# A two-block layer kernel: the norm's factor ahead of the MLP applied to the gate and up results, input blocks made within the output product

## The reference

```python
def rms_norm(x, g):
    xf = x.astype(jnp.float32)
    y = xf * lax.rsqrt(jnp.mean(xf * xf, axis=-1, keepdims=True) + EPS)
    return (y * g.astype(jnp.float32)).astype(x.dtype)
...
    h = h + m @ w_o
    hn = rms_norm(h, norm2_g)
    gate, up = jnp.split(hn @ w_gate_up, 2, axis=-1)
    return h + (jax.nn.silu(gate) * up) @ w_down
```

## Time and profile before

| | us |
|---|---|
| median of 3 runs | 2365.99 |
| lowest, highest | 2365.02, 2367.89 |
| the profiled execution, its own time | 2365.47 |
| its span in the profile | 2363.7 |
| TensorE busy, share of the span | 2202.0, 93% |
| mean granted clock of TensorE, share of full speed | 0.969 |

### The profile page before, as it was taken

How to read it: one execution, slowest core, us unless ns; L and a number is a source line. 1 busy time by engine, 2 the same in 40 slices (tenths; PEclk the granted TensorE clock), 3 DMA queues, 4 the chain that set the end, 5 groups by cost and what they waited for, 6 DMA issues and landing times.

```text
span 2363.7 us, 29779 instructions
## 1 busy us (share of the span) xinstructions
PE 2202.0 (93%) x10756; PEld 1811.1 (77%) x10756; DVE 1410.7 (60%) x2782; ACT 899.4 (38%) x1609; POOL 1003.0 (42%) x575
## 2 busy tenths in 40 slices
PE   7999999999999989999589999999999798998896
PEld 6877688998887767788368888888888576878774
DVE  4258799999902566661646666665467617307713
ACT  5234522232225754431422333334455333226622
POOL 1355433465452332144465454555488513130042
PEclk9999999999999989999789999999999899999998
DMA  5111111111242121243124444447855121110212
GB/s 181 52 45 68 55 53 52 47 45 45 74 131 90 63 80 37 72 152 124 55 87 156 157 156 157 154 152 251 298 168 169 54 107 36 54 45 15 90 41 89
DMA packets 235366, 233.74 MB, mean 99 GB/s; under 512 B 10194, under 2 KB 177775, under 8 KB 235231
## 3 DMA queue, kind: packets, MB, share of 16 engines
q1 hardware_dynamic: 231072, 218.77, 28.5%
q10 hardware_dynamic: 4158, 13.16, 1.4%
HBM read 169.82 MB, written 61.15 MB: 98 GB/s over the span
## 4 chain that ended last, share of the span: by engine, by line
PE 72%; DVE 9%; ACT 3%; issue 2%; POOL 2%; DMA 1%; SPq 0%; ACTq 0%; DVEq 0%
PE ps L889 23%; PE ps L1177 17%; PE ps L1199 9%; PE ps L1242 8%; PE ps L1066 6%; PE ps L1388 4%; PE ps L1098 1%; POOL xl_P L2836 1%; DVE logit L2106 1%; PE ps L1041 1%; PE ps L1084 1%; ACT p_s L1928 1%; DVE pt_lo L2125 1%; DVE mix L2282 0%; PE ps L1311 0%
## 5 line engine op out<-in xcount | busy, mean ns | idle before, releaser
L2645 POOL TENSOR_TENSOR w_lo<-w_raw,w_hi 128x1024 fp32r<-128x1024 f32 (+1 forms) x135 | 290.8, 2155 | 887.7 <-ACT w_hi L1420 887.7
L889 PE MATMUL ps<-x_hi,w_hi 128*128 128x512 f32 (+2 forms) x960 | 361.6, 377 | 3.3 <-DVE c_rs L2023 3.3
L889 PE MATMUL ps<-x_lo,w_hi 128*128 128x512 f32 (+2 forms) x960 | 360.1, 375 | 0.0
L889 PE MATMUL ps<-x_hi,w_lo 128*128 128x512 f32 (+2 forms) x960 | 358.1, 373 | 0.0
L1177 PE MATMUL ps<-xh_P,wr_hi 128*128 128x512 f32 x616 | 246.5, 400 | 29.9 <-issue 21.9
L1177 PE MATMUL ps<-xl_P,wr_hi 128*128 128x512 f32 x616 | 245.7, 399 | 0.0
L1177 PE MATMUL ps<-xh_P,wr_lo 128*128 128x512 f32 x616 | 245.5, 399 | 0.0
L889 PEld LDWEIGHTS ps<-x_hi,w_hi 128*128 128x128 f32 x960 | 181.7, 189 | 39.1 <-issue 8.4
L889 PEld LDWEIGHTS ps<-x_hi,w_lo 128*128 128x128 f32 x960 | 181.9, 190 | 28.9
L889 PEld LDWEIGHTS ps<-x_lo,w_hi 128*128 128x128 f32 x960 | 181.6, 189 | 28.4
L1420 ACT CAST w_hi<-w_raw 128x1024 fp32r<-128x1024 f32 (+1 forms) x135 | 127.1, 943 | 171.3 <-PE ps L889 83.4
(11 more groups left out here) (405 smaller groups left out, 4910.2 us busy)
## 6 DMA issues: line engine op xcount, KB each, us to landing
w_raw<-in_w_in SPq DMA_DIRECT2D x74, 512.0 KB, 3.6
wdr<-as_scratch SPq DMA_DIRECT2D x77, 256.0 KB, 3.3
rawg<-in_w_gate_up SPq DMA_DIRECT2D x22, 512.0 KB, 3.9
rawu<-in_w_gate_up SPq DMA_DIRECT2D x22, 512.0 KB, 5.3
wdr<-in_w_down SPq DMA_DIRECT2D x22, 512.0 KB, 6.5
as_scratch<-ac SPq DMA_DIRECT2D x44, 256.0 KB, 3.8
wt_scratch<-wdr SPq DMA_DIRECT2D x33, 256.0 KB, 5.0
as_scratch<-a SPq DMA_DIRECT2D x33, 256.0 KB, 3.5
```

What stands on the lines that cost most here:

```text
L889: mm = pe.matmul(ps[:, b, 0:n], w[:, s, P * k:P * k + P], r[:, k, t0:t0 + n], start=k == 0 and i == 0, stop=k == kd - 1 and i == 2 and ext ...
L2645: pool.tensor_tensor(w_lo[:, p % 2, 0:n], w_raw[:, p % 2, 0:n], w_hi[:, p % 2, 0:n], ALU.subtract).then_inc(wlo_done, 1)
```

## The change

- The inputs of the product are no longer multiplied by the norm's factor. ACT scales a tile of `mix` by the gain only (`gained`, in place; the last tile into `gh7`) once SP's store of it has landed (`park_sum`), and does so within the output product, one panel behind. The squares are made by half tile, and summed over tiles in `rsb[0]` and `rsb[1]`.
- Casts of the tiles of P1 and P2 (`x_high`), their low parts and the four sums of each tile pair (`sums`) stand within the output product too; `combined_weights(0)` and six `block_low` are there as well. The sums reuse other tiles than before. The blocks are placed elsewhere, and `xtr` has two buffers instead of four.
- TensorE sums and spreads the squares in one step (two matmuls of `ones` with `rsb`, behind P2 of pair 0). DVE makes the mean and the reciprocal on 128 x 512 numbers (`inverse_rms`), ACT the root, within pair 0.
- In each pair P2 is multiplied by `rsb[0]` ahead of its silu (DVE, `gate`), `g1` by `rsb[1]` ahead of its silu (DVE), and `a[1]` and `a[0]` by `rsb[1]` and `rsb[0]` ahead of the multiplication with `g1` and `g0` (POOL).
- `down_combined(0)` moves from pair 0 to pair 1.

```diff
@@ TensorE
-            norm_sums(0)
-            norm_spread(0)
...
                     if prod == "P7":
-                        pe.wait_ge(po_done, 5 * n + 1)
+                        pe.wait_ge(po_done, 7 * n + 1)
...
+                    if n == 0 and prod == "P2":
+                        pe.wait_ge(acca_done, 14)
+                        for h in range(2):
+                            pe.matmul(ps[:, 6 + h, :], ones[:, :], rsb[h][:, :], start=True, stop=True).then_inc(rs_full, 1)
@@ ACT
+            def gained(m):
+
+                act.wait_ge(park_store[m % 2], PARK_0[m % 2] + 16 * (m // 2 + 1))
+                act.wait_ge(sqa_done, 2 * m + 2)
+                act.activation(mix[:, m, :], mix[:, m, :], ACT.Copy, scale=v("norm2_g", m)).then_inc(hn_done, 1)
...
+                square(m, 0)
+                if m:
+                    gained(m - 1)
+                    x_high(m - 1)
...
+                    if n == 0 and i == 3:
+                        act.wait_ge(nst_step, 4)
+                        for h in range(2):
+                            act.activation(rsb[h][:, :], rsb[h][:, :], ACT.Sqrt).then_inc(nrt_done, 1)
+                    if i == (at("P2") + 1 if n else 5):
+                        act.wait_ge(po_done, 7 * n + 2)
+                        act.activation(g0[:, :], g0[:, :], ACT.Silu).then_inc(sil_done, 1)
@@ DVE
+            def sums(k):
+                dve.wait_ge(hn_done, scaled_at(4 + k))
+                dve.tensor_tensor(wdr[:, k, :], scaled(k, 1), scaled(4 + k, 1), ALU.add).then_inc(s0_done, 1)
...
+            def inverse_rms():
+                for h in range(2):
+                    dve.wait_ge(rs_full, h + 1)
+                    dve.tensor_scalar(rsb[h][:, :], ps[:, 6 + h, :], 1.0 / D, EPS, ALU.mult, ALU.add).then_inc(nst_step, 1)
+                for h in range(2):
+                    dve.wait_ge(nst_step, h + 1)
+                    dve.reciprocal(rsb[h][:, :], rsb[h][:, :]).then_inc(nst_step, 1)
...
+                def gate():
+                    if n:
+                        dve.wait_ge(am_done, AM_DONE_0 + 4 * n)
+                    else:
+                        dve.wait_ge(nrt_done, 2)
+                    dve.wait_ge(blk_done, BLK_DONE_0 + 7 * n + at("P2") + 1)
+                    dve.tensor_tensor(g0[:, :], bank_of["P2"], rsb[0][:, :], ALU.mult).then_inc(po_done, 1)
...
+                        dve.tensor_tensor(g1[:, :], g1[:, :], rsb[1][:, :], ALU.mult).then_inc(po_done, 1)
@@ POOL
-                    if i == 3 and n % 2 == 0:
+                    if (n, i) == (1, 1) or i == 3 and n % 2 == 0 and n:
                         down_combined(n // 2)
                     if i == 5:
+                        pool.wait_ge(po_done, 7 * n + 4)
+                        pool.tensor_tensor(a[1][:, :], a[1][:, :], rsb[1][:, :], ALU.mult).then_inc(am_done, 1)
+                        pool.wait_ge(am_done, AM_DONE_0 + 4 * n + 1)
                         pool.wait_ge(sil_done, 2 * n + 2)
                         pool.tensor_tensor(a[1][:, :], a[1][:, :], g1[:, :], ALU.mult).then_inc(am_done, 1)
                     if i == 6:
-                        pool.wait_ge(po_done, 5 * n + 5)
+                        pool.wait_ge(po_done, 7 * n + 7)
+                        pool.tensor_tensor(a[0][:, :], a[0][:, :], rsb[0][:, :], ALU.mult).then_inc(am_done, 1)
+                        pool.wait_ge(am_done, AM_DONE_0 + 4 * n + 3)
                         pool.tensor_tensor(a[0][:, :], a[0][:, :], g0[:, :], ALU.mult).then_inc(am_done, 1)
```

More of the change, by code:

```diff
@@ L325, in build @@
         gy_s = place("gy_s", [P, 2, BANK], F32, ST + 20 * S)
-        n_acc = place("n_acc", [P, 1, S], F32, ST)
-        n_sq = place("n_sq", [P, 2, 2, S], F32, ST + 8 * S)
+        n_sq = place("n_sq", [P, 2, BANK], F32, ST + 8 * S)
+        rsb = [place("rsb0", [P, BANK], F32, RA + 30 * S), place("rsb1", [P, BANK], F32, W_RAW + 6 * KD * P * 4 + 32 * S)]
+        gh7 = place("gh7", [P, S], F32, ST + 24 * S)
         n_diag2 = place("n_diag2", [P, S], F32, ST + 8 * S)
@@ L668, in half, with scaled, scaled_at, sum_at @@
             return slice(BANK * h, BANK * h + BANK)
+        def scaled(m, h):
+            return gh7[:, half(h)] if m == KD - 1 else mix[:, m, half(h)]
+        def scaled_at(m, h=1):
+            return HN_DONE_0 + m + 1 + (h if m == KD - 1 else 0)
+        SUMS = ("S1", "S3", "S2", "S4")
+        def sum_at(name, k):
+            return S0_DONE_0 + 4 * k + SUMS.index(name) + 1
+        def block_tile(y):
+            prod, k = FIRST[y // 4], y % 4
+            return prod, k, {"P1": scaled(k, 0), "P2": scaled(4 + k, 0), "P4": scaled(4 + k, 1), "P5": wdr[:, k, :],
+                             "P6": scaled(k, 0), "P7": scaled(k, 1), "P3": scaled(4 + k, 0)}[prod]
+        IN_SET = {"P1": 1, "P2": 1, "P6": 0, "P7": 0, "P5": 3, "P3": 3, "P4": 2}
         block = ctx.enter_context(nc.Block())
@@ L758, in _ @@
                     sp.wait_ge(olo_done, 8)
-                    for n in range(4):
-                        load_residual(n)
+                    load_residual(0)
+                    load_residual(1)
                 if kind == "wo" and m >= 4:
-                    load_residual(2 * m - 4)
-                    load_residual(2 * m - 3)
+                    load_residual(2 * m - 6)
+                    load_residual(2 * m - 5)
+                    park_sum(m - 4)
                 if key == ("wo", 1):
@@ L769, in _ @@
                     load_pair(0)
[L771 to L775, removed]
+            for m in range(4, KD):
+                if m < KD - 1:
+                    load_residual(2 * m + 2)
+                    load_residual(2 * m + 3)
+                park_sum(m)
             load_pair(1)
             def store_inner(j):
-                sp.wait_ge(am_done, AM_DONE_0 + 4 * j + 4)
+                sp.wait_ge(am_done, AM_DONE_0 + 8 * j + 8)
                 sp.wait_ge(ac_done, AC_DONE_0 + 4 * j + 4)
@@ L1798, in _ @@
                         block_high(q)
-            norm_split()
+            gained_last(1)
+            for y in range(8, 12):
+                x_high(y)
             for n in range(FC):
@@ L2279, in normalized @@
-            def normalized(z):
-                m, h = PIECES[z]
-                dve.wait_ge(rs_full, h + 1)
-                dve.scalar_tensor_tensor(out=mix[:, m, half(h)], in0=mix[:, m, half(h)], scalar=v("norm2_g", m), in1=ps[:, 6 + h, :],
-                                         op0=ALU.mult, op1=ALU.mult).then_inc(hn_done, 1)
-            dve.wait_ge(hs_store, 16 * KD)
-            for z in range(8):
-                normalized(z)
-            for y in (1, 3):
-                x_low(y)
```

288 lines of the change are left out of this document (147 added, 141 removed).

## The result

The changed kernel takes 2404.24 us (median of 4 runs, 2401.08 to 2406.75) against 2365.51 us of the kernel before on the same chip: ratio 1.0164, 95% interval 1.0146 to 1.0181. It is slower by 38.7 us; the prediction was 2402.0, range 2355 to 2422.

A forecast was written before the change was run, and what follows sets the result against it. TensorE, 93% busy, was taken to bound the kernel: only its gaps can give time, and new gaps are paid in full. 2365.5 - 13.9 - 7.2 + 57.6 = 2402.0 us, range 2355 to 2422.

The forecast's parts named there:

- Ahead of the pairs: From the output product's end through pair 0: 49.5 us instead of 63.45, -13.9 us, bounds -18 and -8.
- Pair 1: Second MLP pair: P7 has no wait, so 19.5 us instead of 26.7, -7.2 us, bounds -7.2 and -3.
- The ring: Dependency loop over two pairs: +5.85 us less 1.75 of slack makes P7 wait 4.1 us in odd pairs 3 to 19.
- a: POOL from down_combined to the low part of block 7n+12: 9.5 us, predicted to grow by 1.85.
- b: DVE's combined_weights and the sum of P6 behind it: 5.1 us, predicted to grow by 1.1.
- d: From the pair's end to POOL's low part of block 7n+6: 5.6 us, predicted to grow by 2.9.
- e: SP's load_pair and wdr loads, from that low part until POOL starts: 8.9 us, predicted unchanged.
- Piece c: TensorE's P7, P4 and P3 in the odd pair: 8.4 us, predicted unchanged.
- The turns of DVE and POOL: Inside the pairs, two-input DVE and POOL instructions alternate on one port: wait 4.1 us; without this 2.05.
- The clock: TensorE's clock falls anew behind each of nine P7 waits in odd pairs 3 to 19, costing 2.3 us each.
- Stalls, clock stays up: Rival: the nine P7 waits cost 4.1 us each without clock falls, 2381 us; chance 0.17.
- the pairs hold: Rival: inside the pairs additions stay under 1.5 us, P7 never waits, 2344.4 us; chance 0.17.

The follow-up runs named there:

- the run without the first wait: Changed kernel without TensorE's wait for all 16 half sums ahead of pair 0: 2403.43 us, ratio 1.0165.
- the one with the reciprocals moved: Changed kernel, pair 0: DVE's inverse_rms and gate moved behind the sum a[1] of P7, ACT's roots from i = 3 to i = 5: 2408.86 us, ratio 1.0179.
- The experiment one pair ahead of the waits: Changed kernel without POOL's two multiplications by rsb in the odd pairs: 2368.70 us, ratio 1.0014.
- the run without the factor: Changed kernel without POOL's two multiplications and DVE's one of g1 by rsb from pair 2 on: 2351.26 us, ratio 0.9953.
- exchanging two groups of DVE instructions: Changed kernel, from pair 1 on DVE adds P6 to r1 ahead of combined_weights for the next pair: 2364.41 us, ratio 1.0005.
- the sum first in the kernel before: Kernel before, from pair 1 on the sum of P6 put ahead of combined_weights: 2372.48 us, ratio 1.0013.
- the low part of block 15: Against the 2360.23 us version with reordered sums and roots: DVE makes pair 1's low part of block 15 behind the sums of P7; 2361.05 us, ratio 0.9972.
- `wdr` early: Changed kernel, SP issues the wdr loads of even pairs ahead of its low-part waits and load_pair: 2398.33 us, ratio 1.0148.
- the run without DVE's part: Changed kernel without DVE's multiplication of g1 by rsb[1] from pair 2 on: 2385.7 us, one run.

## Why the prediction was right, and where it was not

It was right in sign, in size (+36.5 us expected, +38.7 measured) and in its main mechanism, and some of the agreement is luck: three terms were off and partly cancelled.

- *Ahead of the pairs*: -13.9 expected, -10.2 measured (63.45 to 53.2). The mis-sized term is DVE's queue ahead of P7's sum, which ended 43.0 us after the product instead of 39.5; what stands behind it took 10.2 instead of 10. It was late from its start. The last half sum was done at 10.2 instead of 8.8, and the low parts of the input tiles up to the 19th at 24.9 (the row of 1161.80) instead of 20.6, several of them at 1.7 us each beside POOL's. The two reciprocals measured 6.54, as estimated (3.3 each) from the 6.65 of 1040 columns. Ahead of them DVE was idle for 1.77 us at 1167.51, waiting for ACT: ACT's casts of P7 stood behind the cast of block 7, which waited for `combined_weights(1)`. P1 also started later, at 10.3 instead of 8.9, which by itself cost nothing, as the run without the first wait shows. That run and the one with the reciprocals moved show that this whole part is one queue: taking one piece out frees little.
- *Pair 1*: 19.5 expected, 19.6 measured.
- *The ring*: the pieces were a +1.85, b +1.1, d +2.9, e 0. In pairs 6 to 8 they measure a +1.7 (11.2 against 9.5), b +1.0 (6.1 against 5.1), d +2.3 (7.9 against 5.6), e -0.2 (8.7 against 8.9). Piece c took 10.3 us: 8.4 of matmuls, 1.5 of the clock's fall, and the rest at its ends. The wait of 4.1 us became 3.7 on average. The experiment one pair ahead of the waits puts d at 1.9. The nine pairs were the right ones.
- *The turns of DVE and POOL*: right for the ring. DVE's 0.68 became 1.67 and 1.77 there beside POOL's multiplications. The Trainium skill, SBUF — State Buffer, section "Who interferes with whom", says that the shared port pair is an exclusive lock and that, outside the two-port modes, a DVE instruction with at most one SBUF input doesn't contend. The traces agree with the second half: POOL took 1.27 us beside the reciprocals of the changed kernel, and 1.71 beside DVE's low parts where the reciprocals were moved. But the earlier trace rows, which the prediction took for turns, show something else. The first of the two POOL instructions alone stood for 15.46 us (1169.74 to 1185.20), while 23 DVE instructions with two inputs followed each other at 0.67 us each, and it ended only after DVE had waited for a result of its own, at 1184.1. The stretch in between, in the kernel before (columns as in the earlier trace rows; DVE is the third number after the length, POOL the fifth):

```profile
1170.14:1184.06 13.92, 2.37 (x6) 1.94 (x7) 13.92 (x24) 10.88 (x18) 13.92 (x1) 0.50 0.00 0
```

So an unbroken queue of DVE kept POOL out for many instructions: one engine at a time, but not by turns. A lock held for one instruction at a time would have let POOL in sooner; here the measurement decides. Where the low parts met with the reciprocals moved, the two did take turns; what decides between the two cases no run here shows. The case for turns thus rested on two right rows (1.67 and 1.68) and on one that was misread.

- *The clock*: 2.3 us each from the earlier trace rows; measured 1.5 in the stretch shown, and at most 1.9 on average (19.4 us for ten falls, one of them twice as long as the others, with what the shown waits leave out). The single row that I used was a longer fall. "Stalls, clock stays up" (2381) is refuted for waits of this length.
- *Not foreseen*: the wait of P3 in pair 20 (3.2 us and a fall). I had followed the ring through the load of `wdr`, but not asked what happens where the load is early. With it, the part inside the pairs is 33.5 + 3.2 + 19.4 = 56.1 against 57.6 expected. It stands in for the 0.4 us by which each of the nine waits was shorter than forecast, and this is the luck in that term.
- The sum: -10.2 - 7.1 + 56.1 = +38.8, and +38.7 is what the medians show.

That the pairs hold (2344) would have needed 1.5 us or less of additions; the run without the factor is the nearest to that kernel, at 2351.

## What to carry to other kernels

When an engine is busy without gaps, follow the ring that sets the slack of each wait all round, queues of DMA issues included, and set additions anywhere on it against that slack: work one pair ahead counted 1.9 of its 2.5 us. Where a wait appears, look first at what stands ahead of the awaited instruction in its engine's own queue: exchanging two groups of DVE instructions gave back some 40 us, more than leaving out DVE's multiplication or POOL's two in odd pairs. But a gain in one pair was given back further on three times here (roots later, the sum first in the kernel before, the low part of block 15), so read each stage by itself before a gain is counted.

## What the runs showed of the hardware that I had not expected

The clock goes with about a third of what the short waits cost (19.4 of 56.1 us). Behind waits of 3.1 us and more it fell nearly each time (ten of ten in the changed kernel, eight of ten with `wdr` early). Behind the seven waits of 1.6 to 2.0 us of the run with POOL's part left out in odd pairs it fell once, though they recur in the same way: 1.00 in the stretch behind the wait of 1.64 us, 0.62 behind that of 2.00. Length alone doesn't decide it: in the run without DVE's part it stayed up behind a wait of 3.44 us and fell behind two of 2.85. The Trainium skill, TensorE: Matmul & The Clock Gate, section "HAM oscillation — how this bites in real kernels", describes a loop in which the wait of each pass brings the clock down anew; the nine of the changed kernel agree. The short ones here are shorter than the waits of its example and mostly left the clock up. So the 1.9 us taken off a wait were worth some 3.2 (33.7 us less 4.7 for pair 20, by nine).

An unbroken run of two-input instructions on DVE held one POOL instruction for 15.46 us in the kernel before, as told above. A long instruction with one operand (6.54 us for the two reciprocals) is also a window in which POOL runs undisturbed. Taking it out of a queue gave back less than its length, because the two-operand work of the two engines then met.
